# A decoder step whose prologue is replanned: query product and scores by column quarters, and the ring of expert rows begun two pairs further on

## The chip, the cores and the metric

The kernel runs on one core of one Trainium2 chip. The metric is the device time of one launch in microseconds, and lower is better. The core has a matmul engine (TensorE, PE in the profile, with PEld for its weight loads), VectorE (DVE), ScalarE (ACT), GpSimd (POOL), and SyncE (SP), which here only issues transfers. Transfers run on 16 DMA engines. Two queues matter: SP's, and POOL's for indirect gathers.

## The reference

One decoder layer over a prompt of 1024 tokens (with 16 meta tokens ahead) and 8 sequences of 8 new tokens against a cache of 1024. Cut to what matters here:

```python
xp = xp + mixer_output(lat, ro, rg, w_uv, w_out)       # attention and retention, d = 1024
h  = rmsnorm(xp, g_ffn)
q  = (h @ w_q).reshape(tokens, 8, 2, 64)               # 8 heads, two halves
sc = einsum('thpd,hpnd->thpn', q, sub_keys)            # 128 scores for each half
s1, i1 = top_k(sc[:, :, 0], 16); s2, i2 = top_k(sc[:, :, 1], 16)
top_s, ci = top_k(s1[..., :, None] + s2[..., None, :], 16)
e    = i1[ci // 16] * 128 + i2[ci % 16]                # 16 experts for each head: 128 for each token
gate = softmax(top_s)
out  = sum over (h, k) of gate * gelu(u_tab[e] . h) * v_tab[e]
```

Every token reads 128 rows of `u_tab` and 128 of `v_tab` (1024 float32 each). The kernel keeps the two tables side by side, so one expert is one row of 8 KB. All arithmetic is float32.

## The kernel before, in words

**Tiles and slots.** The tokens stand in nine tiles of 128: tile 1 to 8 are the prompt, tile 9 the samples. Beside them there is a "raw" tile 0, which holds the sample tokens and the meta tokens. A *slot* is one expert choice of all 128 tokens of a tile: 128 slots for each prompt tile, 64 for the last, 1088 in all (`NSLOT`). For slot s, POOL gathers 128 rows of 8 KB (1 MB) into a pair of rows of the buffer `R` (`pair(s)`, L257, a ring of `RN` = 8 pairs), DVE multiplies the u half with `hb` and sums it (L1600), ACT applies gelu and the gate and writes a diagonal matrix (L1223, L1225, L1230), and PE adds diagonal times v half to the two PSUM banks of `Y` (L972, four instructions of 512 columns, two matmuls). Gather s waits until PE has done with slot s - 8.

**The plan.** `plan()` (L95) writes by hand one order of work, which every engine follows in its own instruction stream. `first` is what runs ahead of slot 0. `turns[g]` is what runs at turn g, ahead of slot g on POOL and DVE, slot g - 1 on ACT and slot g - 2 on PE (`LAG` = 2). An engine never goes past an instruction that waits. `spread(items, lo, hi)` lays parts evenly over turns lo to hi - 1; `mixed(a, b)` interleaves two lists. The parts: `prep` (norm, transposes and gain of a token tile), `items` (the input projection: one item is one tile by one chunk of 256 columns of `w_in`, 16 PE instructions on L679), `kv`, `q`, `att`, `ret` (mixer of a tile), `out`, `norm2`, `query` (output product L918, norm, query product L945, transposes L645, scores L956, copies to `SC` L1206), `top` (sorting on DVE from L1528 on; its `gd` exponential is on ACT, L1216), `lda` and `ldb` (a parked projection comes back from `prd` in DRAM into `pr`).

**Buffers.** The ten chunks of `w_in` of the first pass lie in `R[2c:2c+2]`, in the same place as pair c of the ring. The four buffers for the weights `w_out` and `w_query` of tile 1 are `R[0:4]` (`w_buf`, L310), each a block of 128 rows by 1024 columns. Slot 0 therefore waits on POOL (L623) until the whole query product is done, and slots 0 to 7 each until the last item with their chunk. The scores of all eight heads of tile 1 are made together, and `top(1, 0)`, which sorts heads 0 and 1, waits for them (L1206 `sc1`). `top(1, 1)` to `top(1, 3)` sort two heads each, at turns 0 to 60.

**The opening.** The input of tile 1 is asked for first (`px0`), then `ident`, `gcol` and chunks 0 and 1 of `w_in`, then the raw tile (`px1`, sample rows and meta tokens). In `first`, `prep(0)` (tile 1) and `prep(1)` (raw tile) are mixed part by part, and items 0 to 3 follow: (chunk 0, tile 1), (chunk 1, tile 1), (chunk 1, tile 0), (chunk 2, tile 1). The first pass has 30 items.

Of the kernel before, what the change touches and what calls it, by code (L numbers as in the profile page):

```python
# [15 lines left out]
P = 128  # L16
D = 1024
NCH = D // P
# [42 lines left out]
for (_c, _t), _k in PARKED.items():  # L61
    INTO[_k] = (_c, _t)

PARTS = dict(prep=6, kv=5, q=6, att=37, ret=12, out=11, norm2=4, query=13, top=20, meta=4, atts=68, rets=21, lda=1, ldb=1,
             lds=27)
# [29 lines left out]
def plan():  # L95
# [8 lines left out]
    prep = lambda n: [x for j in range(len(PASSES[n])) for x in stage("prep", 4 * n + j)]  # L104
    tail = lambda t: stage("out", t) + stage("norm2", t) + stage("query", t)
    it = stage("items", 0)
    first = mixed(stage("prep", 0), stage("prep", 1)) + it[0:4]
    first += stage("kv", 0) + stage("kv", 1) + stage("q", 1) + mixed(stage("att", 1), stage("prep", 2) + it[4:17])
    first += stage("meta", 0) + mixed(stage("ret", 1), it[17:21])
    first += tail(1)[0:10] + it[21:22] + tail(1)[10:]  # L110
    first += stage("lda", 2) + mixed(top(1, 0), it[22:27])
    spread(it[27:], 0, 4)
    spread(stage("kv", 2) + stage("q", 2), 0, 8)
    for piece in range(1, 4):
# [5 lines left out]
    for t in range(1, NTILE):  # L120
        at = P * (t - 1)
        if t > 1:
            spread(top(t, 1), at, at + 40)
        spread(stage("att", t + 1) + stage("ret", t + 1), at + (5 if t > 1 else 9), at + 60)
        spread(stage("ldb", t + 1), at + 36 if t > 1 else 8, at + 37)
        spread(tail(t + 1), at + 60, at + 90)
        spread(top(t + 1, 0), at + 90, at + 118)
        if t + 2 <= NTILE:
            spread(stage("lda", t + 2), at + 64, at + 65)
            spread(stage("kv", t + 2) + stage("q", t + 2), at + 96, at + 128)  # L130
# [21 lines left out]
def build(nc, A, marks):  # L152
# [3 lines left out]
    with ctx:  # L156
# [66 lines left out]
        def bank(b, lo=0, hi=512):  # L223
            return PS[:, 512 * b + lo:512 * b + hi]
# [29 lines left out]
        def ones(n):  # L254
            return krg[32 * n + 32:32 * n + 33, 512:512 + P]

        def pair(s):  # L257
            return R[:, 2 * (s % RN):2 * (s % RN) + 2, :].rearrange("p a d -> p (a d)")

# [50 lines left out]
        def w_buf(t, m):  # L310
            return R[:, m % 4, :] if t == 1 else wring[:, m % 2, :]

        names = ["dve", "act", "pe", "pool"] + [f"uv{i}" for i in range(RN)] + \
# [58 lines left out]
        def _(e):  # L372
# [182 lines left out]
            def out(p, t):  # L555
                nb = w_bufs(t)
                yield from p.to(0)
                for m in range(nb):
                    load_w(t, m, p)
                for m in range(nb, NCH + nb):  # L560
                    yield from p.to(3 + m - nb)
                    load_w(t, m, p)

            def query(p, t):
# [30 lines left out]

            run(dict(prep=prep, items=items, kv=kv, lda=lda, ldb=ldb, lds=lds, atts=atts, rets=rets, out=out, query=query), peer)
            for s in ("kv_out", "y0", "y1", "st_out"):
# [4 lines left out]
        def _(e):  # L602
# [16 lines left out]
            def peer(s):  # L619
                if s >= NSLOT:  # L620
                    return
                t = tile_of(s)
                if s == 0:  # L623
                    e.wait_ge(pe_done, c.at("pe", f"used q1_{NCH - 1}"))
                if s < RN:
                    e.wait_ge(pe_done, c.at("pe", f"P0_{max(i for i, x in enumerate(ITEMS[0]) if x[0] == s)}"))
                else:
                    e.wait_ge(pe_done, c.at("pe", f"v{s - RN}"))
                if s == P * NTILE:
                    e.wait_ge(dve_done, c.at("dve", "idxS"))  # L630
# [8 lines left out]
        def _(e):  # L639
# [43 lines left out]
            def kv(p, t):  # L683
# [4 lines left out]
                if t >= 2:  # L688
                    e.wait_ge(act_done, c.at("act", f"sc{t - 1}"))
                e.transpose(bank(5, 0, P), ckv_of(t), ident[:])  # L690
# [245 lines left out]
            def query(p, t):  # L936
# [21 lines left out]
                m.then_inc(pe_done, c.count(f"sc{t}"))  # L958

            def peer(g):  # L960
                s = g - LAG
# [9 lines left out]
                for n in range(2):  # L971
# [3 lines left out]

            run(dict(prep=prep, items=items, kv=kv, meta=meta, q=q, att=att, ret=ret, atts=atts, rets=rets, out=out, norm2=norm2,
                     query=query), peer)


        @block.scalar  # L980
        def _(e):
# [212 lines left out]
            def query(p, t):  # L1194
# [10 lines left out]
                for s in range(2):  # L1205
                    act(SC[:].rearrange("p (h s x) -> p s h x", h=H, s=2)[:, s, :, :],  # L1206
                        two(2 + 3 * s).rearrange("p (h x) -> p h x", h=H), ACT.Copy).then_inc(
                            act_done, c.count(f"sc{t}" if s else None))

            def top(p, k):  # L1210
                t, piece = k // 4, k % 4
# [6 lines left out]
            def peer(g):  # L1218
# [12 lines left out]
                for t in range(1, SMP + 1):  # L1231
                    if g == last_slot(t) + LAG + 1:
# [3 lines left out]

            run(dict(prep=prep, items=items, kv=kv, q=q, att=att, ret=ret, atts=atts, rets=rets, out=out, norm2=norm2, query=query,
                     top=top), peer)


        @block.vector
        def _(e):
# [253 lines left out]
            def top(p, k):  # L1496
# [208 lines left out]
```

## Time and profile before

| | us |
|---|---|
| median of 3 runs | 3562.11 |
| lowest and highest | 3547.14, 3569.12 |
| the profiled execution | 3551.95 |
| its span, first to last instruction | 3550.2 |
| mean granted TensorE clock | 0.962 |

The profile is that of one execution. Its span is 1.75 us below its time. Busy shares are sums over the whole span, in which three stages differ: the opening up to the first gather, the long loop over slots with the next tiles' mixer between them, and the end.

### The profile page before, as it was taken

Reading aid. Unit: us, or ns where it says so; the run is one execution under the profiler, and the core shown is the slowest. Engines: PE = TensorE matmul, PEld = TensorE weight load, DVE = VectorE, ACT = ScalarE, POOL = GpSimd, SP = SyncE. Lnnn points to the kernel's source line nnn. Section 1 sums busy time; section 2 is a strip of 40 time slices with the busy share of each in tenths; the row PEclk is TensorE's granted clock in tenths of the full one; section 3 lists DMA queues with packets and bytes.
Section 4 is the critical chain, followed back from the end, with each engine's and each line's share of the span. In section 5 each row is a group of like instructions: output and inputs, shape, how many; then the busy total and the mean of one; then the engine's idle time right before and its main releaser. Section 6 shows DMA issues by size and latency. Waiting matters only on the chain.

```text
span 3550.2 us, 33864 instructions
## 1 busy us (share of the span) xinstructions
PE 3170.8 (89%) x10190; PEld 1613.1 (45%) x10190; DVE 2105.7 (59%) x5347; ACT 1612.3 (45%) x4383; POOL 1270.6 (36%) x1097
## 2 busy tenths in 40 slices
PE   6989999998989998998999889988898888978887
PEld 5655555543445444554445334543354344533222
DVE  1256637675576457663767477656755376645954
ACT  2146324554455344652556345644564355423433
POOL 0023324343443334342434344334334343323442
PEclk8999999999999999999999999999999999989999
DMA  4269989999999999999999999999989998889998
GB/s 172 92 268 359 383 341 408 391 408 411 372 420 360 399 375 418 371 394 364 406 403 377 402 400 421 337 400 396 420 314 390 354 367 313 331 314 356 411 422 351
DMA packets 234350, 1295.00 MB, mean 365 GB/s; under 512 B 45700, under 2 KB 66084, under 8 KB 91446
## 3 DMA queue, kind: packets, MB, share of 16 engines
q0 software_dynamic: 156672, 1140.92, 80.4%
q1 hardware_dynamic: 77494, 151.92, 11.6%
q8 instruction: 80, 1.31, 0.1%
q14 instruction: 104, 0.85, 0.1%
HBM read 1275.74 MB, written 16.44 MB: 364 GB/s over the span
## 4 chain that ended last, share of the span: by engine, by line
PE 56%; DMA 24%; DVE 12%; ACT 4%; SPq 2%; issue 2%; POOL 0%; DVEq 0%; ACTq 0%
PE PS L972 30%; DMA R<-in_t_uv,idx 8%; PE PS L679 7%; DMA wring<-in_w_out 6%; DVE R L1600 5%; DMA wring<-in_w_query 4%; DMA R<-in_t_uv,idxS 3%; PE PS L918 3%; PE PS L945 3%; PE PS L645 3%; PE PS L760 2%; PE PS L759 2%; PE PS L741 2%; SPq L376 2%; DMA R<-in_cache_krope 1%
## 5 line engine op out<-in xcount | busy, mean ns | idle before, releaser
L972 PE MATMUL PS<-R,diag 128*128 128x512 f32 x4352 | 2055.1, 612 | 158.4 <-ACT diag L1230 116.2
L612 POOL DMA_INDIRECT R<-in_t_uv,idx x1024 | 1206.2, 1178 | 2158.0 <-PE PS L972 1834.2
L1600 DVE CUSTOM_DVE_ANT_0 R<-R,hb 128x1024 f32<-128x1024 f32 x1088 | 1316.5, 1221 | 765.8 <-DMA R<-in_t_uv,idx 682.4
L972 PEld LDWEIGHTS PS<-R,diag 128*128 128x128 f32 x4352 | 802.1, 194 | 1168.8 <-issue 756.2
L1223 ACT ACTIVATE acts<-dots 128x1 f32<-128x1 f32 x1088 | 215.2, 198 | 865.1 <-DVE dots L1600 862.6
L1230 ACT ACTIVATE diag<-ident,wv 128x128 f32<-128x128 f32 x1024 | 411.3, 402 | 248.0 <-PE PS L972 216.1
L1225 ACT ACTIVATE wv<-gate,acts 128x1 f32<-128x1 f32 x1024 | 301.4, 294 | 33.2
L679 PE MATMUL PS<-R 128*128 128x256 f32 (+1 forms) x1280 | 284.9, 378 | 16.6 <-DMA R<-in_t_win 11.3
L679 PEld LDWEIGHTS PS<-R 128*128 128x128 f32 x1280 | 240.1, 194 | 76.9 <-issue 35.7
L918 PE MATMUL PS<-wring,T 128*128 128x512 f32 x256 | 143.2, 688 | 90.9 <-DMA wring<-in_w_out 90.0
L1341 DVE CUSTOM_DVE_ANT_0 PP<-PS,mask 128x144 f32<-128x144 f32 (+7 forms) x64 | 49.5, 773 | 247.4 <-PE PS L760 247.2
L945 PE MATMUL PS<-wring,T 128*128 128x512 f32 x256 | 131.0, 637 | 46.8 <-DMA wring<-in_w_query 46.6
L1223 ACT ACT_TABLE_LOAD x120 | 154.0, 1283 | 2.1
L918 PEld LDWEIGHTS PS<-wring,T 128*128 128x128 f32 x256 | 51.2, 212 | 167.6 <-DMA wring<-in_w_out 95.5
L945 PEld LDWEIGHTS PS<-wring,T 128*128 128x128 f32 x256 | 47.9, 197 | 117.4 <-DMA wring<-in_w_query 71.2
L612 POOL DMA_INDIRECT R<-in_t_uv,idxS x64 | 62.8, 982 | 93.1 <-PE PS L972 89.5
L760 PE MATMUL PS<-krg,T 32*128 32x512 f32 (+4 forms) x224 | 95.3, 504 | 0.0
L1528 DVE MAX8 val<-SC 128x8 f32<-128x128 f32 x288 | 59.6, 278 | 59.7 <-ACT SC L1206 57.9
L1485 DVE TENSOR_TENSOR xb<-PS,xb 128x1024 f32<-128x1024 f32 x9 | 11.0, 1225 | 134.8 <-PE PS L918 134.8
L759 PE MATMUL PS<-ckvT,B 128*128 128x512 f32 (+4 forms) x224 | 89.2, 479 | 1.1 <-ACT B L1071 1.1
L1600 DVE DVE_READ_ACCUMULATOR2_ANT dots<- 128x1 f32 x1088 | 89.5, 82 | 0.0
L741 PEld LDWEIGHTS PS<-scr,ckvR 128*128 128x128 f32 x576 | 74.4, 193 | 24.5 <-issue 21.8
(235 smaller groups left out, 2352.1 us busy)
## 6 DMA issues: line engine op xcount, KB each, us to landing
wring<-in_w_out SPq DMA_DIRECT2D x64, 512.0 KB
wring<-in_w_query SPq DMA_DIRECT2D x64, 512.0 KB
R<-in_t_win SPq DMA_DIRECT2D x27, 1024.0 KB, 18.7
R<-in_t_uv,idx POOLq DMA_INDIRECT x1024
prd<-stg SPq DMA_DIRECT2D x66, 128.0 KB
pr<-prd SPq DMA_DIRECT2D x8, 976.0 KB
xb<-in_x_prompt SPq DMA_DIRECT2D x8, 512.0 KB, 4.0
R<-in_w_out SPq DMA_DIRECT2D x8, 512.0 KB, 5.3
```

Of the source, the lines that this page charges most:

```text
L612: e.indirect_dma_start(dst, None, table, bass.IndirectOffsetOnAxis(ap=index, axis=0)).then_inc(S[s], c.count(name, s, 16))
L679: m = mm(p_bank(n, i)[:, 0:hi - lo], p_xT(n, j)[:, P * q:P * q + P], w[:, q, :], start=q == 0, stop=q == NCH - 1)
L741: mm(bank(7, 0, P), ckvR[:, P * k:P * k + P], scr[:, P * k:P * k + P], start=k == 0, stop=False)
L759: mm(PS[:, S0 + lo:S0 + hi], B1[:, P * h:P * h + P], ckvT[:, lo:hi], start=True, stop=False)
L760: m = mm(PS[:, S0 + lo:S0 + hi], T1[0:ROPE, P * h:P * h + P], krT[:, lo:hi], start=False, stop=True)
L918: m = mm(bank(2 + n), T1[:, P * k:P * k + P], w[:, 512 * n:512 * n + 512], start=k == 0, stop=k == NCH - 1)
L945: m = mm(bank(2 + n), T1[:, P * k:P * k + P], w[:, 512 * n:512 * n + 512], start=k == 0, stop=k == NCH - 1)
L972: m = mm(bank(n), diag[:, s % DR, :], pair(s)[:, D + 512 * n:D + 512 * n + 512], start=begins, stop=s == last_slot(t), skip_group_check=True)
L1223: act(acts[:, k:k + 1], dots[:, k:k + 1], ACT.Gelu).then_inc(act_done, c.count())
L1225: act(wv[:, k:k + 1], gate_of(v), ACT.Copy, scale=acts[:, k:k + 1]).then_inc(act_done, c.count())
L1230: act(diag[:, v % DR, :], m[:], ACT.Copy, scale=wv[:, k:k + 1]).then_inc(act_done, c.count(f"d{v}"))
L1600: e.tensor_tensor_reduce(u, u, hb[:, tile_of(g) % 2, :], 1.0, 0.0, ALU.mult, ALU.add, dots[:, g % NW:g % NW + 1]).then_inc(dve_done, c.cou ...
```

## The change

- The query product, its transposes and its scores of tile 1 are done in four quarters. Quarter j (`quart(p, j)`) covers 256 columns of `w_query`, which are heads 2j and 2j + 1. Its weights come as one transfer of 1 MB into `R[0:2]` (j even) or `R[2:4]` (j odd), in pieces of 1 KB.
- `top(1, j)` waits for the scores of quarter j alone (`sc1_j`).
- Quarter 0 stands where the whole query part stood. Quarter 1 is mixed with items 22 to 25 and `top(1, 0)`. Quarters 2 and 3 are spread over turns 3 to 8.
- Slot s takes pair (s + 2) mod 8 (`home`), so that slots 0 to 5 lie above the weight quarters; slots 6 and 7 wait for quarters 2 and 3.
- Item 26 moves from `first` to turn 0. `kv(2)` and `q(2)` move from turns 0 to 7 to turns 9 to 16, and `att(2)` and `ret(2)` begin at turn 17 where they began at turn 9 (they still end at turn 60).
- In the opening, `prep(0)` and items 0 and 1 stand ahead of `prep(1)`.

```diff
-    tail = lambda t: stage("out", t) + stage("norm2", t) + stage("query", t)
+    tail = lambda t: stage("out", t) + stage("norm2", t) + (stage("query", t) if t > 1 else stage("quart", 0))
-    first = mixed(stage("prep", 0), stage("prep", 1)) + it[0:4]
+    first = stage("prep", 0) + it[0:2] + stage("prep", 1) + it[2:4]
-    first += stage("lda", 2) + mixed(top(1, 0), it[22:27])
-    spread(it[27:], 0, 4)
-    spread(stage("kv", 2) + stage("q", 2), 0, 8)
+    first += stage("lda", 2) + mixed(top(1, 0), it[22:26] + stage("quart", 1))
+    spread(it[26:], 0, 4)
+    spread(stage("quart", 2) + stage("quart", 3), 3, 9)
+    spread(stage("kv", 2) + stage("q", 2), 9, 17)
-        spread(stage("att", t + 1) + stage("ret", t + 1), at + (5 if t > 1 else 9), at + 60)
+        spread(stage("att", t + 1) + stage("ret", t + 1), at + (5 if t > 1 else 17), at + 60)
+        def home(s):
+            return (s + 2) % RN
+
         def pair(s):
-            return R[:, 2 * (s % RN):2 * (s % RN) + 2, :].rearrange("p a d -> p (a d)")
+            return R[:, 2 * home(s):2 * home(s) + 2, :].rearrange("p a d -> p (a d)")
...
+            def load_quarter(j):
+                e.wait_ge(pe_done, c.at("pe", f"used q1_{j - 2}" if j >= 2 else f"used o1_{5 + 2 * j}"))
+                w = A["w_query"].rearrange("o (c p) n -> p (o c) n", p=P)
+                dma(w_quarter(j), w[:, :, 256 * j:256 * j + 256], f"w{2 * (j % 2)}", f"q1_{j}")
...
-                if s == 0:
-                    e.wait_ge(pe_done, c.at("pe", f"used q1_{NCH - 1}"))
-                if s < RN:
-                    e.wait_ge(pe_done, c.at("pe", f"P0_{max(i for i, x in enumerate(ITEMS[0]) if x[0] == s)}"))
+                if s < RN and home(s) < 2:
+                    e.wait_ge(pe_done, c.at("pe", f"used q1_{home(s) + 2}"))
+                elif s < RN:
+                    e.wait_ge(pe_done, c.at("pe", f"P0_{max(i for i, x in enumerate(ITEMS[0]) if x[0] == home(s))}"))
...
+            def quart(p, j):
+                yield from p.to(0)
+                if j == 0:
+                    e.wait_ge(act_done, c.at("act", "hT1"))
+                if j >= 2:
+                    e.wait_ge(act_done, c.at("act", f"qq1_{j - 2}"))
+                e.wait_ge(S[f"w{2 * (j % 2)}"], c.at(f"w{2 * (j % 2)}", f"q1_{j}"))
+                for k in range(NCH):
+                    m = mm(bank(2 + j % 2, 0, 256), T1[:, P * k:P * k + P], w_quarter(j)[:, k, :],
+                           start=k == 0, stop=k == NCH - 1)
+                m.then_inc(pe_done, c.count(f"used q1_{j}"))
+                yield from p.to(2)
+                e.wait_ge(act_done, c.at("act", f"qq1_{j}"))
+                transposes(lambda i: scr[:, 256 * j + P * i:256 * j + P * i + P], 2,
+                           lambda i: bank(7, P * i, P * i + P)).then_inc(pe_done, c.count(f"qqT1_{j}"))
+                yield from p.to(4)
+                e.wait_ge(act_done, c.at("act", f"qqT1_{j}"))
+                for i in range(2):
+                    h = 2 * j + i
+                    for f in range(2):
+                        m = mm(bank(5 + f, P * i, P * i + P), B1[64 * f:64 * f + 64, P * h:P * h + P],
+                               keysT[64 * f:64 * f + 64, h, :], start=True, stop=True)
+                m.then_inc(pe_done, c.count(f"sc1_{j}"))
...
+            def quart(p, j):
+                cols = slice(256 * j, 256 * j + 256)
+                yield from p.to(1)
+                e.wait_ge(pe_done, c.at("pe", f"used q1_{j}"))
+                act(scr[:, cols], bank(2 + j % 2, 0, 256), ACT.Copy).then_inc(act_done, c.count(f"qq1_{j}"))
+                yield from p.to(3)
+                e.wait_ge(pe_done, c.at("pe", f"qqT1_{j}"))
+                act(B1[:, cols], bank(7, 0, 256), ACT.Copy).then_inc(act_done, c.count(f"qqT1_{j}"))
+                yield from p.to(5)
+                e.wait_ge(pe_done, c.at("pe", f"sc1_{j}"))
+                for f in range(2):
+                    act(SC[:, 512 * j:512 * j + 512].rearrange("p (h s x) -> p s h x", h=2, s=2)[:, f, :, :],
+                        bank(5 + f, 0, 256).rearrange("p (h x) -> p h x", h=2), ACT.Copy).then_inc(
+                            act_done, c.count(f"sc1_{j}" if f else None))
...
-                e.wait_ge(act_done, c.at("act", f"sc{t}"))
+                e.wait_ge(act_done, c.at("act", f"sc{t}" if t > 1 else f"sc1_{piece}"))
```

## Rows read from the trace of the kernel before

**Rows 1.** The page's busy times: us, share of span, instructions.

```profile
PE 3170.8 (89%) x10190; PEld 1613.1 (45%) x10190; DVE 2105.7 (59%) x5347; ACT 1612.3 (45%) x4383; POOL 1270.6 (36%) x1097
```

**Rows 2.** Stretches: length; busy us of PE, PEld, DVE, ACT, POOL; clock, DMA share, GB/s.

```profile
226.00:247.00 21.00, 21.00 (x68) 10.34 (x67) 14.13 (x56) 8.98 (x28) 6.97 (x7) 0.87 1.02 422
...
260.00:280.00 20.00, 16.88 (x54) 8.88 (x54) 19.35 (x45) 18.76 (x42) 6.24 (x5) 0.91 1.02 422
280.00:294.00 14.00, 14.00 (x51) 7.38 (x50) 13.11 (x52) 13.52 (x31) 5.28 (x5) 1.00 0.98 375
...
312.00:345.00 33.00, 33.00 (x114) 19.20 (x115) 20.25 (x50) 23.43 (x61) 13.66 (x11) 1.00 0.84 312
345.00:384.00 39.00, 39.00 (x137) 23.52 (x136) 29.17 (x103) 18.66 (x59) 13.55 (x14) 1.00 0.98 379
```

**Rows 3.** The chain that ended last, opening: start us, us, what.

```profile
3.72 12.21 DMA SC<-in_meta_tokens
...
21.31 15.02 PE PS L679 x64
```

**Rows 4.** Timeline, opening: start, us, engine, line, operation, [idle before <-releaser].

```profile
8.26 1.11 PE L645 MATMUL PS<-ident,xb 128*128 128x128 f32 x4 [8.26 <-DVE xb L1282]
...
18.46 1.11 PE L645 MATMUL PS<-ident,SC 128*128 128x128 f32 x4 [9.09 <-DVE SC L1282]
...
47.95 0.66 PE L645 MATMUL PS<-ident,scr 128*128 128x128 f32 x4 [1.09 <-ACT scr L1056]
```

**Rows 5.** The same columns, from the start to 10.5 us.

```profile
0.00:10.50 10.50, 1.11 (x4) 0.71 (x4) 0.92 (x2) 4.01 (x5) 1.63 (x9) 1.00 0.78 257
```

**Rows 6.** Timeline, from the query product to the first gather.

```profile
162.35 3.62 PE L679 MATMUL PS<-R 128*128 128x256 f32 x16
...
170.70 17.06 PE L945 MATMUL PS<-R,T 128*128 128x512 f32 x32 [1.11 <-ACT T L1192]
...
188.87 1.09 PE L645 MATMUL PS<-ident,scr 128*128 128x128 f32 x8 [1.11 <-ACT scr L1197]
...
191.07 2.06 PE L956 MATMUL PS<-keysT,B 64*128 64x128 f32 x32 [1.11 <-ACT B L1200]
...
195.00 0.39 ACT L1015 ACTIVATE stg<-PS 128x256 f32<-128x256 f32 x1
195.15 0.87 DVE L1528 MAX8 val<-SC 128x8 f32<-128x128 f32 x4 [26.71 <-ACT SC L1206]
```

**Rows 7.** Timeline, from the first gather on.

```profile
213.43 1.08 POOL L612 DMA_INDIRECT R<-in_t_uv,idx  x1 [211.14 <-DVE gate L1578]
...
219.54 1.23 DVE L1600 CUSTOM_DVE_ANT_0 R<-R,hb 128x1024 f32<-128x1024 f32 x1 [3.74 <-DMA R<-in_t_uv,idx]
...
225.62 3.78 PE L972 MATMUL PS<-R,diag 128*128 128x512 f32 x4 [6.79 <-ACT stg L1015]
...
229.68 1.40 POOL L612 DMA_INDIRECT R<-in_t_uv,idx  x1 [5.62 <-PE PS L972]
```

**Rows 8.** Timeline, ScalarE, an exponential and the next tile load's first reader.

```profile
251.06 1.28 ACT L1103 ACT_TABLE_LOAD   x1
252.36 0.52 ACT L1103 ACTIVATE PP<-PP,small 128x272 f32<-128x272 f32 x1
...
255.15 1.04 ACT L1000 ACTIVATE R<-R 128x1024 f32<-128x1024 f32 x1
```

**Rows 9.** Groups by line, TensorE, 226 to 432 us: busy us, mean ns, idle before.

```profile
L760 PE MATMUL PS<-krg,T 32*128 32x272 f32 x16 | 5.8, 440 | 0.0
...
L770 PE MATMUL PS<-ident,PP 128*16 128x128 f32 x8 | 2.2, 273 | 0.0
```

**Rows 10.** SyncE's transfers from 233.5 to 235.2 us (one prd load, three prompt tiles).

```profile
L376 SPq DMA_DIRECT2D R<-in_x_prompt x3: 425/432/432, 233.8 to 234.7; - x3
...
DMA to landing us min/median/max: 12.7/16.0/19.2
```

**Rows 11.** The chain that ended last, turn 26: start us, us, what.

```profile
294.21 10.57 DMA R<-in_t_win
```

More of the change, by code:

```diff
@@ L62 @@
     INTO[_k] = (_c, _t)
-PARTS = dict(prep=6, kv=5, q=6, att=37, ret=12, out=11, norm2=4, query=13, top=20, meta=4, atts=68, rets=21, lda=1, ldb=1,
+PARTS = dict(prep=6, kv=5, q=6, att=37, ret=12, out=11, norm2=4, query=13, quart=6, top=20, meta=4, atts=68, rets=21, lda=1, ldb=1,
              lds=27)
@@ L311, in w_buf, with w_quarter @@
             return R[:, m % 4, :] if t == 1 else wring[:, m % 2, :]
+        def w_quarter(j):
+            i = 2 * (j % 2)
+            return R[:, i:i + 2, :].rearrange("p a d -> p (a d)").rearrange("p (c n) -> p c n", c=NCH)
         names = ["dve", "act", "pe", "pool"] + [f"uv{i}" for i in range(RN)] + \
@@ L559, in out @@
                     load_w(t, m, p)
-                for m in range(nb, NCH + nb):
+                for m in range(nb, NCH + (nb if t > 1 else 0)):
                     yield from p.to(3 + m - nb)
                     load_w(t, m, p)
+                if t == 1:
+                    yield from p.to(7)
+                    load_quarter(0)
+                    yield from p.to(9)
+                    load_quarter(1)
+            def load_quarter(j):
[3 more added lines that the diff above has]
+            def quart(p, j):
+                if j < 2:
+                    yield from p.to(1)
+                    load_quarter(j + 2)
             def query(p, t):
@@ L594, in load_x @@
                     dma(xb[:, t % 2, :], x_rows[P * (t - 1):P * t, :], f"xb{t % 2}", f"x{t}")
-            run(dict(prep=prep, items=items, kv=kv, lda=lda, ldb=ldb, lds=lds, atts=atts, rets=rets, out=out, query=query), peer)
+            run(dict(prep=prep, items=items, kv=kv, lda=lda, ldb=ldb, lds=lds, atts=atts, rets=rets, out=out, query=query, quart=quart),
+                peer)
             for s in ("kv_out", "y0", "y1", "st_out"):
@@ L688, in kv @@
                 if t >= 2:
-                    e.wait_ge(act_done, c.at("act", f"sc{t - 1}"))
+                    e.wait_ge(act_done, c.at("act", f"sc{t - 1}" if t > 2 else "sc1_3"))
                 e.transpose(bank(5, 0, P), ckv_of(t), ident[:])
@@ L976, in _ @@
             run(dict(prep=prep, items=items, kv=kv, meta=meta, q=q, att=att, ret=ret, atts=atts, rets=rets, out=out, norm2=norm2,
-                     query=query), peer)
+                     query=query, quart=quart), peer)
         @block.scalar
@@ L1208, in query, with quart @@
                             act_done, c.count(f"sc{t}" if s else None))
+            def quart(p, j):
+                cols = slice(256 * j, 256 * j + 256)
+                yield from p.to(1)
+                e.wait_ge(pe_done, c.at("pe", f"used q1_{j}"))
[9 more added lines that the diff above has]
+                            act_done, c.count(f"sc1_{j}" if f else None))
             def top(p, k):
@@ L1237, in _ @@
             run(dict(prep=prep, items=items, kv=kv, q=q, att=att, ret=ret, atts=atts, rets=rets, out=out, norm2=norm2, query=query,
-                     top=top), peer)
+                     quart=quart, top=top), peer)
         @block.vector
```

## The prediction

> **What bounds the kernel now.** I read the page first: TensorE is busy for 3170.8 of 3550.2 us, DVE for 2105.7, ACT for 1612.3 [rows 1]. Then the stretches show that the bound changes early in the loop. From 226 to 280 us the DMA engines are full (share 1.02 at 422 GB/s) while from 260 to 294 DVE and ACT are nearly full too (19.35 and 18.76 of 20 us); from 312 to 384 PE has no idle time (33.00 of 33, 39.00 of 39) and DMA has a little left [rows 2]. After the opening all is relative: each wait is on another engine or on a slot, none on a clock. So whatever lead the opening gives is kept to the end, as far as it is still there when PE has become the bound, around turn 60. The question is what lead is left there.
>
> Two chains are attacked. In the opening, the chain goes from 3.72 us through the meta tokens' transfer (12.21 us) to 64 PE instructions of the first four items, 15.02 us [rows 3]; PE stood still for 9.09 us before the raw tile's transposes [rows 4]. Later, 24.45 us go by from the start of the query product (170.70) to the first sort (195.15), and the first gather is at 213.43, 18.28 us after that [rows 6, 7].
>
> **Opening.** Tile 1's transposes begin at 8.26 and take 1.11 us for four; the second four and the DVE halves follow, so item 0 could start near 11.3. Its chunk must have landed: by 10.5 us 257 GB/s have brought 2.70 MB [rows 5], and the first tile (0.52), `ident`, `gcol` and both chunks (2.10) are 2.69 MB. Chunk 0 is thus there, chunk 1 about when item 1 wants it. An item takes 3.46 us at the full clock (16 of 0.216; the row has 3.62 with the last one's drain [rows 6]). Four transposes took 1.11 us at 8.26 and 18.46 but 0.66 at 47.95 [rows 4]: TensorE was at the half clock at first, whatever the row of that stretch says. The four items took 15.02 for 4 x 3.46 = 13.84, so 1.2 were lost to it, which puts the rise at 23.7, 5.2 us after 18.46. If it again takes 5.2 us of dense work, from 11.3 to 16.5, 2.6 are lost: items 0 and 1 end at 11.3 + 6.9 + 2.6 = 20.8. The raw tile's eight transposes with DVE's halves end at 22.7 and items 2 and 3 at 29.6, for 36.33 before: **6.7 us**. From below: both items wholly at half clock, 2.7. From above: no such loss, 8. What follows (the latent chain of both tiles, `q(1)`) depends on these four items and on transfers that landed earlier.
>
> **First gather.** Quarter 0 needs 8 matmuls of 256 columns, as one item: 3.46 us. Before, the 32 instructions took 17.06 where 13.7 is the full-clock time, so the first 3.4 us of work ran at half clock after PE's short rest; I keep that loss: 6.6. Then a copy of 256 columns (0.39), two transposes (a quarter of 1.09), a copy (0.39), eight score instructions (a quarter of 2.06) and two copies (0.75) [rows 6], with hand-overs 9.2 us in place of 24.45: 15.2 us. The sort itself does not change. First gather: 213.43 - 15.2 - 6.7 = 191.5, 21.9 earlier. The weights: quarter 0 is asked for after `used o1_5`, some 11 us before it is needed, quarter 1 near the end of the output product. In pieces of 1 KB they are twice one of today's 512 KB loads; even at twice the time they are hidden.
>
> **First v product.** PE must do, from the query product's start: 6.6 + 1.6 (rest of quarter 0), items 22 to 25 (13.84), quarter 1 (3.46 + 3.0, since `qqT1_1` stands on ACT behind `gd`'s exponential and its table load of 1.28 [rows 8]), items 26 to 29 (13.84) and a copy (0.4): 42.7. So v of slot 0 starts at 170.7 + 42.7 - 6.7 = 206.7 for 225.62 now. Of the 18.9, 6.8 is PE's idle time before it [rows 7], gone, and the rest is the opening and the two quarters put off. The page "ScalarE: Activation LUTs" of the Trainium skill, section "What ACT_TABLE_LOAD costs", adds 1.38 us of drain to each 1.28 us load, which would make it 208.1 and my gain 1.4 less; here the exponential starts at 252.36, 0.02 after the load ends [rows 8], so I leave it out.
>
> **What is owed after it.** Quarters 2 and 3 (2 x 3.46, and 1.6 of transposes and scores) now stand between v products. Slot 6's gather waits for quarter 2, behind v0: 206.7 + 2.0 + 3.5 = 212.1. Slot 7's waits for quarter 3, behind v3: about 222. The DMA queue, which had six gathers from 191.5 (six times 2.5 us), runs dry in between for some 8 us, partly filled by the parked `pr` load. v7 comes at about 229.8 where it came 8 slots after 225.62, at 247: a lead of 17.
>
> `kv(2)` and `q(2)` now stand in turns 9 to 16, and SyncE's loads of three prompt tiles (turn 12) are in line behind `kv(2)`'s stores, which wait for DVE at turn 9 or 10. They were issued at 233.8, right after a 976 KB load, and landed 12.7, 16.0 and 19.2 us later [rows 10]; the second and third landed 3.3 us later each after an issue 0.5 later, some 3.75 us for 512 KB, which gives 5 to 6 us for the first without the big load ahead. I expect the issue at 237 and the landing at 242.3. ACT, which reads it first and was there at 255.15 [rows 8], would stand before it for about 2 us: lead 12.8. The rest of the way to turn 26 ACT has `q(2)` more and 0.8 head of `att(2)` less, 0.4 us. There PE waits for chunk 0 of the next pass, 10.57 us from its issue [rows 11], as before: lead 12.4.
>
> From turn 26 PE is the bound and has more to do than before. Of 49 parts of `att(2)` and `ret(2)`, 16 were done by then (17 turns of 51) and now 10 are (9 of 43): six parts, 1.5 heads. A head costs PE 3.5 us (seven groups, the first 5.8, the last 2.2, in sum 28.2 for eight heads [rows 9]), so 5.3 at most; pipelining and idle stretches behind 384 us may halve that. I take 4.0. **Sum:** 12.4 - 4.0 = 8.4, rounded to 8 us less.
>
> **Against which time.** The profiled execution took 3551.95, its own time would be 3544. The three runs and this one have the mean 3557.6 and spread over 22 us; I forecast the new median from it: 3557.6 - 8 = **3550**. The first gather's 21.9 us, all kept, are 0.6%.
>
> **Rivals.** (A) *All is kept.* DMA and DVE, not PE, set the pace later too, and the 21.9 us of the first gather stay: 3536. For it: DMA is at 0.98 even from 345 to 384 [rows 2]. Against: PE has no idle time there. (B) *Nothing is left.* The half clock eats the opening (2.7 in place of 6.7) and PE pays all 5.3 after turn 26, with two more us in the waits of the quarters: 2.7 + 5.7 - 5.3 - 2 = 1, so 3557. For it: PE is full from 312 on. (C) *Slower: the prompt tiles are late.* ACT halts at turn 12 until the first tile is there, with DVE, PE and then POOL behind it. Landing L us after an issue at 237, the lead is 255.15 - 237 - L, of which 4.4 are used up later: it decides at L = 13.8. The rows have 12.7 to 19.2 [rows 10]; at 19.2 the kernel is 5.5 us slower, 3563. Against it: the 12.7 contained the 976 KB load. (D) The change does not do what it says, since POOL waits for something else: then the first gather stays near 206 and the lead is the opening's less what PE pays, 6.7 - 4.0, 3555; this lies between my own case and B.
>
> **How the numbers follow.** My case (4 to 15 us less, 3543 to 3554) 0.5, A 0.16, B 0.22, C 0.12. The measured median adds some 8 us to either side. The range 3532 to 3566 takes in A and C's worst and leaves out about 2 in 10. A measurement of this kernel can tell about 1%, 36 us, from no change; none of the cases reaches that, so within 1% has 0.95, and what I have not seen 0.03 for faster, 0.02 for slower.
>
> **What would show it.** Item 0 near 11.3 and item 3's end near 29.6; the first gather near 191.5; v0 near 207 with next to no idle time before it; the seventh and eighth gathers at about 212 and 222 with a gap of DMA between; ACT's first read of a prompt tile near 242 with its releaser a DMA; PE at turn 60 some 8 us earlier than now. I am wrong if the lead at turn 26 is not between 8 and 16 us, or if PE is idle for more than a few us between turns 26 and 60.

## The result, and the profile after

The change made the kernel slower, by a third of a per cent.

| | before | after |
|---|---|---|
| median of 20 runs, us | 3556.18 | 3569.48 |
| lowest and highest | 3545.88, 3576.52 | 3560.09, 3579.01 |
| ratio | | 1.0033, 95% interval 1.0019 to 1.0048 |
| the profiled execution, its span | 3551.95, 3550.2 | 3563.0, 3561.0 |
| mean granted TensorE clock | 0.962 | 0.959 |

The forecast was 3550, within 3532 to 3566. It is wrong in its sign and its range, though everything up to the first gather came as forecast. Later runs of the same kernel put the loss a little lower (0.19 and 0.21%, below), so I speak of a loss of 7 to 12 us.

The page's busy times of the changed kernel answer to [rows 1]. PE's busy time rose by 14.8 us; the work of the other engines is the same.

```profile
PE 3185.6 (89%) x10222; PEld 1627.0 (46%) x10222; DVE 2106.2 (59%) x5347; ACT 1613.9 (45%) x4396; POOL 1265.4 (36%) x1097
```

**The opening**, PE's timeline, to be read beside [rows 3, 4]. Items 0 and 1 (x32) begin at 11.22, items 2 and 3 end at 29.50, for 36.33 before.

```profile
11.22 9.27 PE L703 MATMUL PS<-R,hb 128*128 128x256 f32 x32 [0.87 <-DVE hb L1351]
20.32 1.04 PE L669 MATMUL PS<-ident,SC 128*128 128x128 f32 x8
22.35 3.69 PE L703 MATMUL PS<-R 128*128 128x256 f32 x16 [0.99 <-issue]
25.88 3.62 PE L703 MATMUL PS<-R,hb 128*128 128x256 f32 x16
```

**To the first v product**, timeline, beside [rows 6, 7]: the quarter product, the first gather, the copy of the last item, and slot 0's v product.

```profile
164.48 6.00 PE L992 MATMUL PS<-R,T 128*128 128x256 f32 x16 [1.11 <-ACT T L1240]
...
191.59 1.08 POOL L636 DMA_INDIRECT R<-in_t_uv,idx  x1 [189.29 <-PE PS L669]
...
209.92 0.30 ACT L1063 ACTIVATE stg<-PS 128x160 f32<-128x160 f32 x1 [2.98 <-DMA prd<-stg]
...
210.28 3.56 PE L1020 MATMUL PS<-R,diag 128*128 128x512 f32 x4 [4.10 <-ACT stg L1063]
...
217.57 0.94 POOL L636 DMA_INDIRECT R<-in_t_uv,idx  x1 [18.68 <-PE PS L992]
...
227.24 0.94 POOL L636 DMA_INDIRECT R<-in_t_uv,idx  x1 [8.73 <-PE PS L992]
```

The gather comes at 191.59 (213.43 before), the v product at 210.28 (225.62 before), and the seventh and eighth gathers at 217.57 and 227.24.

**Turn 12** is where the lead ends. ACT's first read of a prompt tile, then its follower on DVE, then the transposes on PE; before, ACT had reached the same instruction at 255.15 [rows 8] without a wait.

```profile
255.13 1.06 ACT L1048 ACTIVATE R<-R 128x1024 f32<-128x1024 f32 x1 [9.55 <-DMA R<-in_x_prompt]
...
257.92 0.16 DVE L1313 RECIPROCAL pst<-pst 128x1 f32<-128x1 f32 x1 [12.47 <-ACT pst L1038]
...
258.93 1.11 PE L669 MATMUL PS<-ident,R 128*128 128x128 f32 x4 [8.86 <-DVE R L1345]
```

The tiles' transfers, SP's instructions by line, beside [rows 10]: issued from 241.30 on, landed 13.8, 17.1 and 20.3 us later.

```profile
L384 SPq DMA_DIRECT2D R<-in_x_prompt x3: 440/450/479, 241.3 to 242.3; - x3
...
DMA to landing us min/median/max: 13.8/17.1/20.3
```

What the DMA engines did meanwhile: the DMA view of 242.0 to 250.5 us, then of 250.5 to 262.6. q0 is POOL's queue of gathers, q1 is SP's.

```profile
q0 software_dynamic: 475, 3.42, 95.5%
q1 hardware_dynamic: 426, 0.15, 6.6%
...
q0 software_dynamic: 486, 3.53, 69.8%
q1 hardware_dynamic: 454, 1.57, 32.2%
```

In both stretches the two queues move about the same *number* of packets: 475 and 426, then 486 and 454. SP's packets were at first the 128 and 512 byte rows of `kv(2)`'s stores (0.15 MB in 8.5 us, 50 a microsecond), then the 4 KB rows of the tiles (37.5 a microsecond, 130 GB/s). These 384 rows, 144 KB, thus held up the tiles behind them for 8.5 us. The Trainium skill, "DMA: Bandwidth & Descriptors", section "Queues, rings and completion order", says that a DMA engine takes turns between queues packet by packet. The counts here fit taking turns. But a packet in the Trainium skill's sense holds some 9 to 17 descriptors, while a packet of the profile here is one row. That a turn is one row, of whatever size, is my reading of these two stretches, and a view further below departs from one for one.

The stretches of [rows 2] in the changed kernel: DMA share fell from 1.02 to 0.86 and 0.81 in the first two, and from 312 to 345 us PE is full again, as before.

```profile
226.00:247.00 21.00, 16.22 (x48) 7.68 (x47) 9.16 (x32) 11.47 (x34) 11.64 (x11) 0.92 0.86 338
260.00:280.00 20.00, 16.86 (x62) 8.72 (x62) 18.43 (x43) 16.53 (x35) 4.67 (x5) 0.84 0.81 297
280.00:294.00 14.00, 13.69 (x47) 6.98 (x46) 13.21 (x44) 12.78 (x28) 4.85 (x6) 0.94 0.89 318
312.00:345.00 33.00, 33.00 (x121) 19.96 (x120) 21.24 (x59) 23.73 (x60) 11.17 (x11) 1.00 0.91 334
```

**Turn 26**, PE's first item on the next pass's first chunk, before and after. The lead of this item is 1.1 us, where I had forecast 12.4. PE's wait shrank from 5.39 to 1.18 us. The item itself took 3.72 us in place of 6.26; before, the granted clock stood at the lower level (1.2 GHz) from 303.2 to 310.0 us.

```profile
304.82 6.26 PE L679 MATMUL PS<-R 128*128 128x256 f32 x16 [5.39 <-DMA R<-in_t_win]
...
303.68 3.72 PE L703 MATMUL PS<-R 128*128 128x256 f32 x16 [1.18 <-DMA R<-in_t_win]
```

**A second place, near the end.** PE's timeline, transposes of the decode cache of one sample sequence. The profile of before has no wait at this place. It has two halts of this kind earlier, the larger one of 8.37 us 137 us before it, the other of 6.23 us 56 us before it. The rows are after, then before.

```profile
3037.78 1.54 PE L669 MATMUL PS<-ident,R 128*128 128x128 f32 x6 [10.05 <-DMA R<-in_cache_krope]
...
2900.75 2.61 PE L645 MATMUL PS<-ident,R 128*128 128x128 f32 x11 [8.37 <-DMA R<-in_cache_krope]
...
2981.50 1.75 PE L645 MATMUL PS<-ident,R 128*128 128x128 f32 x7 [6.23 <-DMA R<-in_cache_krope]
```

### The profile page after: what moved, and what is told of

Its sections match the earlier page's. It is cut to its first block, busy times and chain, and to the rows that moved or that the text cites. A ratio compares the mean times of both kernels' runs of the same rounds, so it can differ in the third digit from the quotient of the medians.

```text
span 3561.0 us, 33939 instructions
## 1 busy us (share of the span) xinstructions
PE 3185.6 (89%) x10222; PEld 1627.0 (46%) x10222; DVE 2106.2 (59%) x5347; ACT 1613.9 (45%) x4396; POOL 1265.4 (36%) x1097
## 4 chain that ended last, share of the span: by engine, by line
PE 56%; DMA 23%; DVE 13%; ACT 5%; issue 1%; SPq 1%; POOL 0%; ACTq 0%; DVEq 0%
PE PS L1020 31%; DMA R<-in_t_uv,idx 7%; PE PS L703 7%; DMA wring<-in_w_out 6%; DVE R L1663 5%; DMA wring<-in_w_query 4%; DMA R<-in_t_uv,idxS 3%; PE PS L942 3%; PE PS L669 3%; PE PS L969 3%; PE PS L784 2%; PE PS L783 2%; PE PS L765 2%; DVE SC L1627 1%; DVE SC L1624 1%
## 5 line engine op out<-in xcount | busy, mean ns | idle before, releaser
L1663 DVE CUSTOM_DVE_ANT_0 R<-R,hb 128x1024 f32<-128x1024 f32 x1088 | 1316.1, 1221 | 780.4 <-DMA R<-in_t_uv,idx 696.3
L1663 DVE DVE_READ_ACCUMULATOR2_ANT dots<- 128x1 f32 x1088 | 89.3, 82 | 0.0
```

The costliest lines, as they stand in the source:

```text
L1663: e.tensor_tensor_reduce(u, u, hb[:, tile_of(g) % 2, :], 1.0, 0.0, ALU.mult, ALU.add, dots[:, g % NW:g % NW + 1]).then_inc(dve_done, c.cou ...
```

## The experiments

To compare profiles I use one figure, the start of DVE's product of slot s (L1600, after L1663), taken from each trace and set against the profile of before: negative is earlier. These are the kernels in the order in which they ran.

| slot | 0 | 8 | 12 | 64 | 768 | 896 | 928 | 1087 |
|---|---|---|---|---|---|---|---|---|
| after | -21.2 | -8.9 | -0.2 | -2.1 | 0.2 | 6.6 | 12.0 | 10.9 |
| tiles_early | -19.6 | -8.1 | -9.3 | -11.5 | -2.3 | 3.6 | 8.9 | 9.6 |
| ring2_only | -1.8 | -2.4 | -2.4 | -2.0 | 6.4 | 8.4 | 11.0 | 11.9 |
| opening_only | -7.1 | -7.2 | -7.3 | -8.5 | -6.1 | -1.4 | 0.5 | -0.7 |
| after_again | -22.2 | -9.8 | -0.6 | 2.1 | 8.9 | 15.8 | 21.4 | 19.9 |
| stores_later | -20.5 | -8.9 | -4.8 | -3.0 | 2.0 | 10.2 | 16.1 | 17.6 |
| rotated | -20.4 | -8.9 | 0.1 | 0.0 | 1.4 | 7.8 | 13.4 | 10.9 |
| old_opening | -14.5 | -2.5 | 6.4 | 5.9 | 15.4 | 23.3 | 28.8 | 27.5 |
| before_again | -0.8 | -0.5 | -0.5 | -0.1 | -3.0 | 2.5 | 1.9 | 1.5 |
| less_before | -1.1 | -1.0 | -1.0 | -1.2 | -5.2 | -5.1 | -13.1 | -10.8 |
| less_after | -21.7 | -9.8 | -0.7 | 0.7 | 6.6 | 13.3 | 5.3 | 5.8 |
| less_tiles | -20.7 | -8.2 | -10.7 | -9.7 | -1.1 | -2.2 | -10.2 | -12.1 |
| ke_opening | -6.3 | -6.2 | -6.2 | -7.0 | -5.1 | -0.1 | -8.1 | -13.7 |
| ke_tiles | -20.0 | -8.4 | -9.0 | -8.9 | 0.7 | 7.3 | -0.1 | -1.3 |

One execution drifts by some 5 us against another between slots 64 and 768, so a single difference of that size tells nothing there; what recurs in every kernel of a kind tells more. The expectations number the theories in the order in which they were formed.

**tiles_early**: the changed kernel, but SP asks for the three prompt tiles at turn 8, behind the parked load, not at turn 12.

```diff
+                if t == 2:
+                    for j in range(3):
+                        load_pass(1, j)
```

> The changed kernel with one thing moved: SyncE asks for the three prompt tiles of the second projection pass at turn 8, right behind the parked projection's load, and no longer behind kv(2)'s stores at turn 12. Theory 1 (the lead is lost because ACT halts 9.55 us at turn 12 for the first of these tiles): the halt is gone, slot 12's u is some 9 us earlier, near 249 us, and the lead over the kernel before at slot 64 is 6 to 10 us where the changed kernel has 2; the time falls by 6 to 10 us against the changed kernel. Theory 2 (TensorE is full from turn 26 on and has more to do there, so the lead would have been lost anyway): the halt is gone but slot 64 is at most 3 us earlier than in the changed kernel, and the time stays.

Measured 3556.27, ratio 0.9986 (0.9969 to 1.0003); after_again, on the same chip, had 3564.01, 7.7 more. The tiles landed 5.7, 6.6 and 7.7 us after an issue at 214.7. The first six gathers had ended by then, and POOL issued the next at 218.08. The 976 KB load of the parked projection (`pr<-prd`) stood right ahead of the tiles here too:

```profile
L384 SPq DMA_DIRECT2D R<-in_x_prompt x3: 333/422/497, 214.7 to 215.5; - x3
L384 SPq DMA_DIRECT2D pr<-prd x1: 320/320/320, 213.9 to 213.9; - x1
...
DMA to landing us min/median/max: 5.7/6.6/7.7
```

ACT reads the first at 246.05 without a wait, and the lead at slot 12 is 9.3 us in place of 0.2. The halt at turn 12 is shown to be the loss of the lead there, and against after_again the 7.7 us are what theory 1 expected. But the lead of 11.5 us over before at slot 64 was worth 5 us in the median (at most 11 by the interval), and in this profile 9.2 us of it are gone at slot 768, so something else takes time later.

**ring2_only**: before, with only the ring moved by two pairs.

```diff
-            return R[:, 2 * (s % RN):2 * (s % RN) + 2, :].rearrange("p a d -> p (a d)")
+            return R[:, 2 * home(s):2 * home(s) + 2, :].rearrange("p a d -> p (a d)")
```

> The kernel before with the ring begun two pairs further on (slot s in pair (s + 2) mod 8) and nothing else; slot 0 still waits for the whole query product. Theory 3 (the place of the pairs costs time in the late stretch, slots 576 to 1087, where the changed kernel lost 12 us): that stretch is 10 to 14 us longer than in the kernel before, and the time is 0.3% longer. Theory 4 (the late loss comes from how transfers fall in time, not from where the pairs lie): no difference beyond 3 us in the time.

Measured 3560.51, ratio 1.0007 (0.9992 to 1.0023). The shift alone costs nothing that the medians can tell (the interval is 5 us to either side). The stretch from slot 576 to 1087 was 7 us longer in its profile, short of the 10 to 14 of theory 3, and it was 6 us longer in before_again too.

**opening_only**: before, with only the new order of the opening.

```diff
-    first = mixed(stage("prep", 0), stage("prep", 1)) + it[0:4]
+    first = stage("prep", 0) + it[0:2] + stage("prep", 1) + it[2:4]
```

> The kernel before with the opening order alone: tile 1's transposes and items 0 and 1 ahead of the raw tile's transposes. If the opening's gain is kept, as nothing behind it has a time of its own, the first gather and slot 64 are both 4 to 7 us earlier and the time is 4 to 7 us less. If the late stretch answers to a shift of a few us by chance, the time can be anywhere within 12 us of the kernel before although slot 576 is 4 to 7 us earlier.

Measured 3552.40, ratio 0.9984 (0.9973 to 0.9994). The opening's 7 us are there from slot 0 to slot 512 (8.3), and the interval of the ratio stays below 1, though this one profile ends only 0.7 us ahead.

**after_again**: the changed kernel once more, on the same chip as the three above.

> The changed kernel as it is, a second profile. If its 12 us in the late stretch belong to the change, the stretch from slot 576 to slot 1087 is again near 1571 us where the kernel before had 1560; if they were that execution's alone, it is nearer 1560 and the time must have another explanation. The halt of ACT at turn 12 should be there again with 8 to 11 us.

Measured 3564.01, ratio 1.0019 (1.0004 to 1.0034). The halt at turn 12 is there again. Slots 576 to 1087 took 1575.5 us, for 1571.3 in the first profile and 1560.3 in before, so the late loss belongs to the change in large part.

**stores_later**: the changed kernel, with the two stores of tile 2's latents (256 rows of 512 and 128 bytes, 80 KB together) put behind the tile loads.

```diff
+                    if n == 1 and j == 2:
+                        stored(2)
...
+                        if t != 2:
+                            stored(t)
```

> The changed kernel, where SyncE puts the two stores of tile 2's latents and keys (256 packets of 512 and 128 bytes, 80 KB) behind the three prompt tiles' loads and not ahead of them; the two copies into ckvR (128 packets of 512 bytes) stay ahead. Theory 5 (beside a full gather queue SyncE's queue gets turns by the packet, some 45 to 50 packets each us whatever their size, and 384 small packets ahead of the first tile cost 8.5 us): 256 packets fewer are 5 to 6 us, the first tile lands 8 to 9 us after its issue and ACT's halt at turn 12 is 3 to 5 us where it was 9.55. Theory 6 (the delay goes by bytes or is the fixed latency of a transfer on a full DMA): 80 KB are 0.2 us, and the halt stays at 9 to 10 us. If the halt's shortening is kept, the time is 4 to 6 us below the changed kernel's.

Measured 3567.44, ratio 1.0020 (0.9999 to 1.0040). The first tile landed 10.3 us after its issue, and ACT's halt shrank from 9.55 to 5.02; theory 5 had 8 to 9 and 3 to 5:

```profile
250.51 1.06 ACT L1055 ACTIVATE R<-R 128x1024 f32<-128x1024 f32 x1 [5.02 <-DMA R<-in_x_prompt]
...
DMA to landing us min/median/max: 10.3/16.8/20.9
```

It landed at 250.48 in place of 255.11, 4.6 us sooner: 1.1 because it was asked for sooner and 3.5 because it landed faster. The row of landings is over five transfers, the two stores among them; the tiles' own are 10.3, 13.4 and 16.8 us, so the second and third came 4.6 us sooner too. The 80 KB would take 0.2 us at 400 GB/s; as 256 small packets at 50 a microsecond they are 5.1. So the delay goes by the number of packets rather than by the bytes, though 5.1 overstates the 3.5 to 4.6 measured. The medians don't resolve the gain of 4.6 us.

**rotated**: the changed kernel, with ring, chunks and weight quarters turned so that slot s lies again where it lay before.

```diff
-            return R[:, 2 * home(s):2 * home(s) + 2, :].rearrange("p a d -> p (a d)")
+            return R[:, 2 * (s % RN):2 * (s % RN) + 2, :].rearrange("p a d -> p (a d)")
```

> The changed kernel with all places of the ring turned back by two pairs: slot s lies where it lay in the kernel before, and the first eight chunks of w_in and the weight quarters are moved with it, so that every wait is the changed kernel's and only addresses differ. Theory 3 (the place of the pairs in SBUF costs time in the loop): 4 to 10 us less than the changed kernel, and the late stretch as in the kernel before. Theory 4 (places don't matter): the time of the changed kernel within 3 us.

Measured 3564.08, ratio 1.0021 (1.0006 to 1.0036), with the halts at turn 12 (11.3 us) and near the end (10.0 us) again. The ratio is that of after_again (1.0019) within 0.0002, so the addresses are not what the medians see as the loss, within some 5 us. One thing stays open. From slot 64 to 768 the nine profiles with the shifted ring lost 2.2 to 9.6 us against before, 7.2 in the mean, and the five with the old places, rotated among them, lost 2.4 at most.

**old_opening**: the changed kernel with the opening of before (the diff of opening_only, backwards).

> The changed kernel with the opening order of the kernel before. The quarters, the ring and the moved parts alone. If the opening's 6 to 7 us are additive, it is 4 to 8 us slower than the changed kernel, 0.4 to 0.6% above the kernel before, slot 0's gather is near 198 us and ACT halts at turn 12 all the same, since tile loads still stand behind the small stores.

Measured 3571.34, ratio 1.0033 (1.0017 to 1.0050). By the ratios this is 5 us slower than after_again and no slower than `after`, so the medians don't settle the 4 to 8 us expected. In the profile all slots from 0 to 12 come 6.4 to 6.7 us later than in `after`, the halt at turn 12 included (ACT goes on at 261.74): the tile loads wait for DVE's `kv(2)`, which moves with the opening, so the opening's gain is *kept* through the halt. It is the quarters' lead that the halt takes: without the new opening the kernel stands 6.4 us behind before at slot 12.

**before_again**: the kernel before, unchanged, as a control.

> The kernel before as it is, for a second profile and as a control of the comparison. The ratio should be 1.000 within its interval. If the 10 us that the changed kernel lost in slots 832 to 1087 are the change's, this stretch is near 802 us again; if the first profile was a lucky one there, it is 806 to 812.

Measured 3561.36, ratio 1.0015 (0.9997 to 1.0032). The control shows how little a ratio of 0.15% means in one comparison. Its slots 832 to 1087 took 805.6 us, for 802.1 in the first profile of before, so that profile was a little lucky there.

**The late loss.** Between slots 896 and 928 all six changed kernels so far took 5.3 to 5.9 us longer than before (after: 6.6 to 12.0), while before_again took 0.6 less, opening_only 1.9 and ring2_only 2.6 more. PE's halt there on `in_cache_krope` was 10.0 to 11.7 us in the six, 6.2 in before, 4.5 in before_again, 6.2 in opening_only and 8.0 in ring2_only. The DMA view of the changed kernel, 3025 to 3036 us, has SP's small packets beside the gathers again, 792 against 588. That is 1.35 for one, so turns of one row each don't describe this stretch:

```profile
q0 software_dynamic: 588, 4.24, 93.6%
q1 hardware_dynamic: 792, 0.22, 8.7%
```

Seen over more slots, the loss is larger. Slots 832 to 1087 took the six 809.4 to 813.7 us (mean 811.4), and the four without the quarters (before, before_again, opening_only, ring2_only) 802.1 to 805.6 (mean 803.5). Of these 7.9 us, 4.5 lie in slots 896 to 928 and 3.9 in slots 832 to 896. In the second stretch PE waits for the weights of `query`: the longest such wait was 11.1 to 13.8 us in the six and 3.9 to 10.9 in the four. That it is the cause is not shown: no experiment takes it away, and before_again, with a longest wait of 3.9, took 4.5 us more than before there. The rows are after, then before:

```profile
2802.59 3.78 PE L969 MATMUL PS<-wring,T 128*128 128x512 f32 x4 [11.50 <-DMA wring<-in_w_query]
...
2796.72 3.78 PE L945 MATMUL PS<-wring,T 128*128 128x512 f32 x4 [7.86 <-DMA wring<-in_w_query]
```

Three kernels without most of the cache loads put a price on the halt. They leave out seven of the eight pages of sequences 2 to 7, so their result for the samples is not the layer's. **less_before**, **less_after** and **less_tiles** are before, after and tiles_early with:

```diff
-                for j in range(lo, hi):
+                for j in range(lo if b < 2 else PAGES - 1, hi):
```

> The kernel before, but of the cache rows of batches 2 to 7 only the last page of eight is loaded, so that its decode attention is computed from the page left there by an earlier batch; nothing else is left out. TensorE's halts on those loads in the last 500 us (8.4 and 6.2 us in one profile of before, 12.9 and 4.5 in the other) should be gone. Both theories: the time falls by 8 to 15 us against the kernel before, to some 3545.

> The changed kernel with the same loads left out. Theory 7 (what the changed kernels lose after slot 64 against the kernel before, some 8 us between slots 768 and 928, are the longer halts on small packets of the cache rows beside the gathers): without the loads it comes within 3 us of less_before, ratio 1.000 plus or minus 0.001, and slots 768 to 928 take the same time in both. Theory 8 (the loss has another cause, the clock or chance, and the halts only go with it): it stays 7 to 12 us behind less_before.

> The changed kernel with the three prompt tiles asked for at turn 8, and the same cache loads left out. Its lead over before at slot 64 was 11.5 us and nothing of it was left at the end. Theory 7: with the late halts gone the lead stays, some 10 us faster than less_before. Theory 8: within 3 us of less_before.

| | median, us | ratio to before | slots 896 to 928, against before |
|---|---|---|---|
| less_before | 3546.69 | 0.9957 (0.9930 to 0.9984) | -8.0 |
| less_after | 3549.33 | 0.9966 (0.9947 to 0.9985) | -8.0 |
| less_tiles | 3540.07 | 0.9942 (0.9919 to 0.9966) | -8.0 |

Without the loads the stretch takes the same time in all three; with them it costs before 8 us and the changed kernels 13.5. So 5.5 us of the difference to before, 4.5 to the mean of the four, lie in this one halt. less_after comes within 2.6 us of less_before, and less_tiles 6.6 us ahead of it, for 10 expected. With 6 to 8 runs each, the intervals of these ratios are some 7 to 10 us to either side, so the medians lean to theory 7 and don't prove it. And theory 7 missed on one point: slots 768 to 928 were to take the same time in less_after and less_before, and less_after took 6.6 us more, 5.9 of them in slots 832 to 896 (with a wait of 14.0 us for the weights of `query` for 8.2). In less_after the same view of 3025 to 3036 us has 4.02 MB of gathers and no row for q1 at all:

```profile
q0 software_dynamic: 546, 4.02, 97.8%
```

**A remedy with nothing left out.** The 128 byte rows of a sequence (`krc`) have a buffer that comes free earlier than that of the 512 byte rows. **ke_opening** (on opening_only) and **ke_tiles** (on tiles_early) ask for them there, half of the packets some six turns ahead of the rest:

```diff
+                    yield from p.to(8 * (b - 2) + 3)
+                    e.wait_ge(pe_done, c.at("pe", f"s krT{b - 2}"))
+                    load_cache(b, what="k")
                     yield from p.to(8 * (b - 2) + 9)
                     e.wait_ge(pe_done, c.at("pe", f"s lat{b - 2}"))
-                    load_cache(b)
+                    load_cache(b, what="c")
```

> The kernel before with the new opening alone, and the 128-byte cache rows (in_cache_krope) of batches 2 to 7 asked for about six turns ahead of the 512-byte ones, as soon as their buffer is free, instead of together with them. Nothing is left out. Theory 9 (what halts TensorE at the end is how many small packets are asked for at one time beside the gathers): the halts on the cache rows between slots 832 and 928 (6.9 and 6.2 us) shrink to under 3 each, slots 896 to 928 take 6 to 10 us less than in the new opening alone, and the time falls by 5 to 10 us, to some 3545, ratio 0.996 plus or minus 0.0015. Theory 10 (the number in one burst does not matter, only their sum): halts and time stay within 2 us.

> The changed kernel with the three prompt tiles asked for at turn 8, and the 128-byte cache rows asked for earlier in the same way. Theory 9: the halts of 10.1 and 7.1 us shrink to under 3 each, 10 to 15 us less than with the early tiles alone (3556), so about 3543, ratio 0.9955 plus or minus 0.0015. Theory 10: about 3556, as with the early tiles alone.

ke_opening measured 3539.83, ratio 0.9952 (0.9923 to 0.9980): faster than both kernels, by 17 us than before, of which the opening alone had given 6. ke_tiles measured 3557.32, ratio 0.9986 (0.9962 to 1.0010). The stretch from 896 to 928 took 8.0 and 7.3 us less than in before. PE's waits from 2990 to 3070 us in ke_opening hold no transfer any more:

```profile
PE PS L977 <- ACT diag L1235: 1.9, 2, 1.5
PE PS L650 <- DVE PP L1442: 0.5, 1, 0.5
```

Of the two halts named in the expectation the later one is gone and the earlier one grew (6.9 to 11.7 us in ke_opening, 7.1 to 11.8 in ke_tiles): there the small rows still halt PE, and theory 9's "under 3 each" is missed by half. In ke_tiles the profile is 14 us better than tiles_early behind slot 768, but the medians show none of it. Its profile lost 6.4 us to tiles_early between slots 64 and 96: PE's idle time, most of it waits for the weights of `out` and `query`, grew by 2.9, and its busy time at a lower granted clock by 3.5. That run is a miss, and one profile doesn't say how often that happens.

## Why the prediction was wrong

**Right.** Opening: 11.22 and 29.50 for 11.3 and 29.6, the gain 6.8 for 6.7. Quarter 0: 164.48 and 6.00 for 6.6. First gather: 191.59 for 191.5. I took the rise of the clock, the landing of chunk 0 and the hand-overs from rows of the same engine in the same state, and they carried over. In quarter 0 two small errors cancelled: it began 0.5 us later than I had it and took 0.6 less.

**First v product, 3.6 too late.** 210.28 for 206.7. The term "and a copy (0.4)" was mis-sized. ACT's last copy into `stg` waited 2.98 us for the store `prd<-stg` of an earlier item, and PE for the copy, 4.10 in all. The stores now ran beside the six gathers that the change had brought forward. Before, PE waited for the same copy, 6.79 us [rows 7], and I booked that time as gone; but there the copy stood behind the first slots' gelu on ACT, and a store had no part in it. The seventh and eighth gathers followed at 217.57 and 227.24 for 212.1 and 222, and the lead at v7 was 11.8 for 17.

**The halt at turn 12: the step that failed.** I put the issue of the tile loads at 237 and the landing 5.3 us later. They were issued at 241.30 and landed 13.8 later; both sizes were wrong (4.3 and 8.5 us), and together they make 12.8 us, which is all of the lead of 12.8 that I had forecast for turn 12. The issue was late since `kv(2)`'s stores waited for DVE (26.6 us in SP's waits) and went first. For the landing I had three rows of before, 12.7, 16.0 and 19.2 [rows 10], and talked the first down to 5.3, on the argument that the 976 KB load ahead of it was the cause. The load ahead costs much only beside the gathers, where SP's queue gets about one packet for one of theirs. The DMA view of before has 125 packets of SP's against 158 of the gathers in 236 to 241 us, 0.98 MB in all; 384 small ones took longer than that. In tiles_early the same load stood ahead, with the gathers paused, and the first tile landed in 5.7. What I had in hand, a full DMA [rows 2] and rows of 12.7 to 19.2, spoke for rival C, which I priced at L = 13.8 as its turning point, for an issue at 237. The measured L was 13.8, after an issue 4.3 us later. The landing of 5.7 us in tiles_early is near my 5.3, but at a place without gathers.

**From turn 26 on: 4.0 us owed, none seen in the lead.** My own sign of being wrong came true, since the lead at turn 26 was 1.1 us and not 8 to 16. From slot 12 to 64 the lead goes from 0.2 to 2.1 in `after`, from 9.3 to 11.5 in tiles_early, and it falls from 0.6 to -2.1 in after_again. Nothing like 4.0 is lost in the mean. The six further parts did come: between these two slots PE is busy for 151.7 us in before and for 153.6 to 156.8 in the six changed kernels. But PE had 11.2 us of idle time there before, the wait of 5.39 at turn 26 in it, and 6.6 to 9.1 in the six. So the parts went mostly into time in which PE had stood still. I had read the full stretches of [rows 2] as the whole way to turn 60, and they are not: PE is idle for 8.0 us between slots 26 and 64 in before, for 2.7 in `after`.

**"Kept to the end": wrong as a rule.** I said that a lead at turn 60 stays to the end. Between slots 896 and 928 PE halts for SP's small packets, and the changed kernels take 5.5 us more there than before; over slots 832 to 1087 it is 7.9 in the mean. With less than 10 us at stake, this stage had to be priced too, and I had not looked at it. The same step failed a second time, then: I had taken it that no wait hangs on a transfer. The halt at turn 12 took the gain away, and this stretch turned it into a loss. Why its halts are longer with the quarters is open: SP's and PE's order of work there is the same. Neither the ring's place (rotated) nor the opening (old_opening) nor the prompt tiles (tiles_early) changes it.

**The sum as measured.** Lead at slot 64 (0 in the mean of `after`, after_again and rotated) and 7.9 us in slots 832 to 1087 make 8 us slower; the three medians give 12, 7 and 7.5 (ratio less 1, times 3557). This is a sum of means over profiles, and it leaves out slots 64 to 832, where single profiles drift.

A shorter sum, the lead at slot 64 and what the kernel takes more from slot 896 to 928, gives for single kernels tiles_early -6 (measured -5), opening_only -6.6 (-5.7), ring2_only +0.6 (+2.5), stores_later +2.9 (+7), old_opening +11.4 (+11.7), less_tiles against less_before -8.5 (-6.6), ke_opening -15 (-17). It misses before_again (-0.7 for +5.3), less_before (-9 for -15), less_after (-7 for -12), `after` (+3.4 for +12) and ke_tiles (-16 for -5). The measured values have intervals of 4 to 10 us to either side, so the matches bear the halts out only roughly.

The clock is the rival that no experiment excludes. The clock records of the traces have 267 us at the lower level (1.2 GHz) in before and 289 in `after`, 263 to 282 in the four kernels without the quarters and 281 to 316 in the six with them, and PE's busy time is 3185.6 for 3170.8. The mean granted clock of the 20 runs of `after` is 0.959, for 0.960 in 35 of before; 0.001 of 3557 us is some 4 us. The lower clock often stands behind a halt, as at turn 26, so this may be a consequence of the longer halts as well as a cause beside them.

**The rivals.** C had the mechanism and the place of the lost lead, and I gave it 0.12; the loss below zero came from late in the kernel, where no rival looked. A and B did not happen, nor D.

## What to carry to other kernels

When a change brings gathers forward, list every transfer on another queue that now runs beside them, and count its packets, not its bytes; here 384 rows of 128 and 512 bytes took 8.5 us beside the gathers, where 125 rows of 8 KB, 0.98 MB, took 5. Ask for what is needed next *ahead of* stores of small rows, and in a stretch where the gathers pause. If the trace has a row for the very transfer, under load, take that row as it stands, and explain it away only with a second row. Then look for late stages whose halts are as large as the gain: a lead of under 10 us did not pass them here.

## What the runs showed of the hardware that I had not expected

Beside a queue that always has work, SP's queue moved 426 packets for 475 of the gathers' (8.5 us), and 454 for 486 (12.1 us), though the packets were 350 bytes and 3.5 KB in the mean, and the gathers' 7.2 KB. Late in the kernel it was 792 for 588 (11 us). Three transfers of 512 KB took 13.8 to 20.3 us to land beside the gathers and behind 384 small rows, and 5.7 to 7.7 us with the gathers paused. Two stores of small rows, 80 KB together, delayed each of them by 4.6 us, some 3.5 of it after its issue.
